# Right one-hots of a dense gate table: twelve tokens in one 16-bit compare, weighted by ScalarE and GpSimd

## What is computed

```
top_s, top_i = lax.top_k(s, 16)                       # s: (token, head, 2, 128)
cand_s = top_s[:, :, 0, :, None] + top_s[:, :, 1, None, :]
fs, fi = lax.top_k(cand_s.reshape(T, 8, 256), 16)
idx = take_along_axis(cand_i, fi)                     # cand_i = first * 128 + second
g = softmax(fs)
a = gelu(einsum('td,thkd->thk', x, u[idx]))
out = einsum('thk,thkd->td', g * a, v[idx])
```

## Time and profile before

| | us |
|---|---|
| median of 3 runs (lowest, highest) | 3995.82 (3994.71, 3996.32) |
| the profiled execution: its own time | 3995.24 |
| the profiled execution: span of its trace | 3993.4 |
| gate stage of layer 0, first DVE instruction of line 1615 to last copy of line 1449 | 780.73 to 892.96 |
| gate stage of layer 1, the same | 2790.94 to 2903.96 |

### The profile page before, as it was taken

One profiled execution on the slowest core, in us unless ns is written; L12 is line 12 of the kernel. 1 busy time (PEld: TensorE's weight loads), 2 busy tenths in 40 slices (PEclk: granted clock), 3 DMA queues, 4 the chain that ended last, 5 costly groups with the idle time before them and its releaser, 6 DMA issues. The chain is left out here.

```text
span 3993.4 us, 55792 instructions
## 1 busy us (share of the span) xinstructions
PE 3761.6 (94%) x20637; PEld 3189.9 (80%) x20637; DVE 3269.3 (82%) x6833; ACT 1769.7 (44%) x2928; POOL 989.6 (25%) x796
## 2 busy tenths in 40 slices
PE   8999999789999999999899898995989999999999
PEld 4546789588999999999754646894889999999998
DVE  5727549998999999999763435399979999999998
ACT  3316522394444444444324545222944444444443
POOL 0000000183333333333100000000933333333332
PEclk9999889799999999999989999897999999999999
DMA  7310030399999999999640000300999999999997
GB/s 294 137 44 10 22 126 2 116 260 424 415 415 408 405 407 404 404 405 404 256 158 22 22 22 19 128 1 22 229 404 415 413 410 406 405 404 405 405 405 299
DMA packets 268270, 1033.70 MB, mean 259 GB/s; under 512 B 147072, under 2 KB 150080, under 8 KB 159936
## 3 DMA queue, kind: packets, MB, share of 16 engines
q0 software_dynamic: 77184, 562.07, 35.1%
q1 hardware_dynamic: 190816, 468.07, 30.9%
HBM read 970.69 MB, written 59.39 MB: 258 GB/s over the span
## 5 line engine op out<-in xcount | busy, mean ns | idle before, releaser
L1696 POOL DMA_INDIRECT gbuf<-in_uv,rows x340 | 514.4, 1513 | 863.9 <-DVE hT L1880 794.1
L1488 POOL TENSOR_SCALAR pqT<-iota,selT 128x128 f32<-128x128 f32 x256 | 205.2, 815 | 1323.0 <-ACT selT L1430 1292.6
L1880 DVE SCALAR_TENSOR_TENSOR hT<-gbuf,act,hT 128x1024 f32<-128x1024 f32 x336 | 416.9, 1282 | 6.0
L1865 DVE SCALAR_TENSOR_TENSOR gbuf<-gbuf,ht 128x1024 f32<-128x1024 f32 x340 | 401.9, 1219 | 11.6 <-DMA gbuf<-in_uv,rows 11.6
L1696 POOL DMA_INDIRECT xT<-in_uv,rows x172 | 256.8, 1493 | 473.2 <-DVE hT L1880 393.4
L1712 PE MATMUL ps<-h0h,U0h 128*128 128x384 f32 x1024 | 344.8, 337 | 7.0 <-DVE U0l L1839 7.0
L1712 PE MATMUL ps<-h1h,U1h 128*128 128x384 f32 x1024 | 345.3, 337 | 6.3 <-DVE U1l L1839 6.3
L1712 PE MATMUL ps<-h1h,U1l 128*128 128x384 f32 x1024 | 344.5, 336 | 0.0
L1712 PE MATMUL ps<-h1l,U1h 128*128 128x384 f32 x1024 | 344.5, 336 | 0.0
L1712 PE MATMUL ps<-h0h,U0l 128*128 128x384 f32 x1024 | 344.5, 336 | 0.0
L1712 PE MATMUL ps<-h0l,U0h 128*128 128x384 f32 x1024 | 344.1, 336 | 0.0
(11 more groups left out here) (386 smaller groups left out, 9016.3 us busy)
## 6 DMA issues: line engine op xcount, KB each, us to landing
ring<-in_u SPq DMA_DIRECT2D x128, 1024.0 KB, 13.0
ring<-in_v SPq DMA_DIRECT2D x128, 1024.0 KB
ring<-in_wts SPq DMA_DIRECT2D x26, 2048.0 KB, 8.8
gates<-ring SPq DMA_DIRECT2D x32, 1536.0 KB, 7.4
ring<-gates SPq DMA_DIRECT2D x64, 768.0 KB
abuf<-in_ada_mid POOLq DMA_DIRECT2D x16, 1024.0 KB, 5.0
xT<-in_ada_late SPq DMA_DIRECT2D x16, 1024.0 KB, 4.9
abuf_c<-in_ada_late POOLq DMA_DIRECT2D x8, 1024.0 KB, 5.0
```

Of the source, the lines that this page charges most:

```text
L1488: last = pool.tensor_scalar(one2[:, r % 2, t, :], iota[:], selT[:, 1, t0 + t:t0 + t + 1], selT[:, 2, t0 + t:t0 + t + 1], ALU.is_equal, ALU ...
L1696: pool.indirect_dma_start(out=slots[m % GSLOTS], out_offset=None, in_=inp[f"uv{l}"], in_offset=bass.IndirectOffsetOnAxis(ap=rows[:, c:c + ...
L1865: v.scalar_tensor_tensor(u, u, 1.0, ht[:, m // P, :], ALU.mult, ALU.mult, accum_out=act4[:, n % 2, m % 2:m % 2 + 1]).then_inc(sem(n_ + "do ...
L1880: v.scalar_tensor_tensor(y, x, w, y, ALU.mult, ALU.add).then_inc(sem(n_ + "acc"), 1)
```

## The change

A new SBUF tensor `sel16` holds the second indices as f16, and a view `numbers` of the score buffer holds 0..127 as f16, each value 12 times over (so that the number is the outer and the token the inner index). One DVE instruction of a step compares all 12 tokens into a double buffer `hot` (a view of the old `eq`, f16) in the order partition, number, token. ACT weights tokens 0 to 3 and GpSimd tokens 4 to 11, each reading `hot` with a stride of 12 values and writing the f32 `one2`; GpSimd does its 8 tokens in one instruction. The compares of lines 1615, 1619 and 1488 go. The wait of TensorE for GpSimd moves behind its fourth product; DVE waits for ACT and GpSimd of step r-2 before it writes `hot`, and for the product of step r-2 only before the left one-hots; ACT waits for that product too.

```diff
 def expert_choice(...)
+        hot = eq[:].rearrange("p a h s k -> p (a h s k)")[:, 0:2 * P * SUB].rearrange("p (b n t) -> p b n t", b=2, n=P)
+        numbers = sc[:, 1].bitcast(F16).rearrange("p i k -> p (i k)")[:, 0:P * SUB].rearrange("p (n t) -> p n t", n=P)
-        SUB, DIRECT, SCALED = 12, 2, 6
+        SUB, SCALED = 12, 4
 TensorE, gate_step(r)
                     pe.wait_ge(sem("gm_one"), r + 1)
-                    pe.wait_ge(sem("gm_pool"), r + 1)
                     pe.wait_ge(sem("gm_scaled"), r + 1)
...
                     for t in range(SUB):
+                        if t == SCALED:
+                            pe.wait_ge(sem("gm_pool"), r + 1)
 ScalarE
                 def evict_sel(tb):
                     act.wait_ge(sem(n_ + "t"), tb + 1)
+                    act.copy(sel16[:, tb * P:(tb + 1) * P], ps[:, 5, P:2 * P])
...
                 def scaled(r):
                     act.wait_ge(sem("gm_eq"), r + 1)
-                    for t in range(DIRECT, DIRECT + SCALED):
-                        at = act.activation(one2[:, r % 2, t, :], one2[:, r % 2, t, :], ACT.Identity,
+                    if r >= 2:
+                        act.wait_ge(sem("gm_mm"), r - 1)
+                    for t in range(SCALED):
+                        at = act.activation(one2[:, r % 2, t, :], hot[:, r % 2, :, t], ACT.Identity,
                                             scale=selT[:, 2, r * SUB + t:r * SUB + t + 1])
...
+                act.copy(numbers, iota[:].unsqueeze(2).to_broadcast([P, P, SUB]))
                 act.copy(iota_ps, iota[:]).then_inc(sem("gm_iota"), 1)
 GpSimd
                 for r in range(STEPS):
-                    t0 = r * SUB
-                    pool.wait_ge(sem(n_ + "selT"), (t0 + SUB - 1) // P + 1)
+                    t0, n = r * SUB + SCALED, SUB - SCALED
+                    pool.wait_ge(sem("gm_eq"), r + 1)
                     if r >= 2:
                         pool.wait_ge(sem("gm_mm"), r - 1)
-                    for t in range(DIRECT + SCALED, SUB):
-                        last = pool.tensor_scalar(one2[:, r % 2, t, :], iota[:], selT[:, 1, t0 + t:t0 + t + 1],
-                                                  selT[:, 2, t0 + t:t0 + t + 1], ALU.is_equal, ALU.mult)
-                    last.then_inc(sem("gm_pool"), 1)
+                    pool.tensor_tensor(one2[:, r % 2, SCALED:SUB], hot[:, r % 2, :, SCALED:SUB].rearrange("p n t -> p t n"),
+                                       selT[:, 2, t0:t0 + n].unsqueeze(2).to_broadcast([P, n, P]), ALU.mult)\
+                        .then_inc(sem("gm_pool"), 1)
 VectorE, gate_step(r)
                     if r >= 2:
+                        v.wait_ge(sem("gm_scaled"), r - 1)
+                        v.wait_ge(sem("gm_pool"), r - 1)
+                    v.tensor_tensor(hot[:, r % 2], sel16[:, t0:t0 + SUB].unsqueeze(1).to_broadcast([P, P, SUB]),
+                                    numbers, ALU.is_equal).then_inc(sem("gm_eq"), 1)
+                    if r >= 2:
                         v.wait_ge(sem("gm_mm"), r - 1)
-                    n = SCALED
-                    v.tensor_tensor(one2[:, r % 2, DIRECT:DIRECT + n],
-                                    selT[:, 1, t0 + DIRECT:t0 + DIRECT + n].unsqueeze(2).to_broadcast([P, n, P]),
-                                    iota_ps.unsqueeze(1).to_broadcast([P, n, P]), ALU.is_equal).then_inc(sem("gm_eq"), 1)
-                    for t in range(DIRECT):
-                        v.tensor_scalar(one2[:, r % 2, t, :], iota_ps, selT[:, 1, t0 + t:t0 + t + 1],
-                                        selT[:, 2, t0 + t:t0 + t + 1], ALU.is_equal, ALU.mult)
                     v.tensor_tensor(one1[:, r % 2, 0:SUB], selT[:, 0, t0:t0 + SUB].unsqueeze(2).to_broadcast([P, SUB, P]),
                                     iota_ps.unsqueeze(1).to_broadcast([P, SUB, P]), ALU.is_equal)\
                      .then_inc(sem("gm_one"), 1)
```

More of the change, by code:

```diff
@@ L1269, in expert_choice @@
     def expert_choice(l, w3, pqT, keysT, selT, rows, gates, steps, sc, s2, cand, c2, vals, idxu, posu, idxp, ranks, posh,
-                      shift, fs, first, eq, tabs, sel, mrow):
+                      shift, fs, first, eq, tabs, sel, mrow, sel16):
         n_ = "ch_"
@@ L1931, in expert_layer @@
                               sb(s2, f"first{l}", [P, 2, 16, 16], F16), sb(s2, f"eq{l}", [P, 2, HP, 16, 16], F16),
-                              sb(s2, f"tabs{l}", [P, 2, HP, 16, 16], F16), sb(s2, f"sel{l}", [P, TB, 2, HP, 16]), sb(s2, f"mrow{l}", [P, 2, 256]))
+                              sb(s2, f"tabs{l}", [P, 2, HP, 16, 16], F16), sb(s2, f"sel{l}", [P, TB, 2, HP, 16]), sb(s2, f"mrow{l}", [P, 2, 256]),
+                              sb(s2, f"selT16{l}", [P, TD], F16))
             def pair(name, shape):
```

## The result

The changed kernel takes 4001.76 us (20 runs), the kernel before 3995.28 in the same comparison: 6.5 us more. The ratio is 1.0015, with a 95% interval of 1.0008 to 1.0022, so 3 to 9 us slower. That has the sign of the forecast and lies inside the range of 3979 to 4062, but it is a third of the size: it lies under the forecast's own range of 4004 to 4055, and within the 0.2% that I had called no change. (The period, 3.43 us, does lie in the 3.37 to 4.3 of the forecast.) The profiled execution has a span of 3999.9 us against 3993.4.

A forecast was written before the change was run, and what follows sets the result against it. In the gate stage all engines and DMA were near their limit; DVE and POOL taking turns would lengthen the period from 3.205 to 3.65 us, adding 10.9 x 2 = 21.8 us to 3995.82: 4018 us, range 3979 to 4062 (forecast's own 4004 to 4055).

The forecast's parts named there:

- Mechanism: Gate stage: POOL's reading and DVE's compare take turns, both reading SBUF; period 3.37 to 4.3 us, chance 0.42.
- POOL's reading: Gate step: DVE's next compare must wait until POOL has read, 2.6 us after POOL's start, at 2.6 ns a value.
- POOL's whole instruction: Gate step: GpSimd's single instruction of 1024 values with two inputs, one strided, takes 3.1 us.
- When POOL lets go: Gate step: DVE's compare can begin 2.6 us after POOL's start, before POOL's 3.1 us instruction ends.
- The sum: Gate stage: 24 steps at 3.65 instead of 3.205 us cost 10.7 us per layer, last six 0.2; 21.8 us in all.
- rival 2: Gate stage: POOL keeps DVE out for its whole duration; period 4.15 us, time 4048; chance 0.13.
- rival 5: Gate stage: compare at one value a cycle, 4066 us, or POOL as slow as eight single instructions, 4204; chance together 0.07.
- The start: Ahead of the gate stage and at its first products: added copies and PE's wait for POOL cost nothing.
- ACT's stride: Gate step: ACT's strided input costs nothing; four weightings at 0.31 us and the copy, about 2.6 us.
- The end: Gate stage's last six steps: 21.9 us against 21.7 imposed by stores; step 30's wait shrinks from 4.33 to about 2.
- Store loop: Gate stage: store landing, copies and weightings take 11.5 us for four steps, so no period under 2.9 us.
- Rival 3: Gate stage: the wait doesn't decide, reading plus compare falls under the store loop; period 2.9 us, time 3982; chance 0.26.

The follow-up runs named there:

- e1: The changed kernel with the compare's numbers 0..127 read from PSUM, so one operand in SBUF; 3989.78 us, ratio 0.9987 to the kernel before.
- e2: The changed kernel with GpSimd weighting only one of its eight tokens, the other seven left out; 3987.43 us, ratio 0.9981 to the kernel before.
- e10: e9 with the numbers 0..127 in PSUM as well; 3982.41 us, ratio 0.9966 to the kernel before.
- e3: The changed kernel with ACT and GpSimd reading `hot` without a stride (one-hots wrong, no work left out); 3981.04 us, ratio 0.9962 to the kernel before.
- e5: The kernel before, plus idle PE products ahead of the gate stage (32 in layer 0, 24 in layer 1); 3993.37 us, ratio 0.9995.
- e6: The changed kernel, plus the same idle PE products ahead of the gate stage as e5; 4000.76 us, ratio 1.0010 to the kernel before.
- e7: e1 with 3 tokens weighted by ACT and 9 by GpSimd; 3982.14 us, ratio 0.9964 to the kernel before.
- e9: The changed kernel with `hot` in three groups of four tokens, read at a stride of 8 bytes; 3980.48 us, ratio 0.9965 to the kernel before.

## Why the prediction was off

- **Mechanism: right.** DVE's compare and POOL's instruction take turns; each engine's own work fell and the period rose. Compare 0.95 us alone: measured 0.95. Handover 0.1: 0.09. Shown by e1, e2 and e10.
- **The term that failed: POOL's reading**, "0.28 + 896 x 0.0026 = 2.6 us", and with it the period of 3.65. Measured: DVE's work begins 2.40 us after POOL's start, and the period is 3.43. The price of 2.6 ns for two inputs with a stride came from no row; it is 2.31 ns (e2 and the changed kernel), and 0.28 + 896 x 0.00231 = 2.35 would have been nearly right. The bound of 2.2 ns from the 0.17 us delay was nearer, by luck, as it is of another instruction.
- **POOL's whole instruction**, "0.79 + 896 x 0.0026 = 3.1 us", measured 2.54. The 0.79 us of line 1488's compare-and-multiply was no fixed cost for this other form, whose 128 values take 0.475 us (e2).
- **When POOL lets go.** I had it let go 0.5 us before its end; it let go 0.14 before (2.40 of 2.54). It is 0.14 in e3 too, where the instruction takes 1.90: POOL starts at 821.54 and ends at 823.44, the compare of 823.05 takes 1.20, so its 0.95 us of work began at 823.30. Over all held compares of steps 2 to 30, in both layers, it is 0.13 to 0.14 us in either kernel. The Trainium skill's whole instruction (SBUF — State Buffer, Who interferes with whom) was nearer for this long one. With 2.54 it gives 2.54 + 0.95 + 0.09 = 3.58 us, against 3.43 measured. It was luck that 0.56 us too much for the instruction and 0.36 too much for the early release cancelled but for 0.2.
- **The sum.** At 3.43 instead of 3.65 the 24 steps cost 5.5 us instead of 10.7 in each layer; that is 10 of the 15 us by which I was too high. At the upper end I made a slip: rival 2 with 3.4 us for POOL's instruction has a period of 4.45 us and by the same sum comes to 4066, as rival 5, so 4062 does not take it in.
- **The start, "Nothing".** This was wrong, and is most of the other 5 us. I compared PE's first product and overlooked that before, DVE lost 2.8 us at step 2 to PE's half clock, while in the changed kernel it loses 0.2. So the copy of step 1 comes 11.0 us after the first compare instead of 12.2 in layer 0 (10.9 instead of 12.2 in layer 1). ACT, which was behind the turns by then, catches up: its next copies follow at 3.0 to 3.2 us for five steps before the period of 3.43 holds, another 1.3 us in each layer. e5 and e6 show it for layer 0.
- **ACT's stride, "costs nothing in my sum".** It costs 0.13 us an instruction. Leaving it out did no harm only because ACT had room; in e1 ACT set the pace.
- **The end.** 21.7 us from step 25 on, as forecast, in layer 0; 22.2 in layer 1. Step 30's copy waited 3.05 us, where I had said about 2. The row names PE, but the product of step 30 had ended at 886.97 + 2.92 = 889.89, and the copy came at 893.36. It was the store again: the one that SP had issued at 881.35 took 11.9 us and landed at 893.28. The DMA share, forecast below 0.9 in the steps, is 0.94.
- **PE's releaser.** I named POOL with 0.7 us; it is DVE's left one-hots with 0.5. The wait for POOL stands ahead of the fifth product, and with 2.54 instead of 3.1 us POOL was done by then: its instruction of 819.86 ended at 822.40, while PE, started at 821.72, came to its fifth product at 822.68.
- **Store loop, 2.9 us.** No mean period over steps 8 to 24 came under it; in e3 and e7 it was 2.98 to 3.11. Rival 3, at 3982, is what these runs reached: its condition, reading plus compare under the stores' pace, was met with 8 bytes of stride or with an operand in PSUM, not by the change as it stands.

## To carry to other kernels

Before moving an operand of a VectorE instruction from PSUM to SBUF, look at what GpSimd does at that time. Here, with two operands in SBUF, VectorE's compare had to wait until GpSimd had read, and GpSimd's next instruction waits for that compare by semaphore: nearly the sum of both durations became a bound. Work out such a bound between the two engines before counting what each one saves alone. And when a layout makes one engine's write dense and others' reads strided, choose the inner group so that the stride is 8 bytes, as in e9; here that turned 6 us of loss into 14 of gain.

## What was unexpected of the hardware

- A 16-bit compare of two tensors is as fast with one of them in PSUM: 0.947 us for 1536 values in e1, 0.951 with both in SBUF in e2. The f32 one of line 1625 takes 1.74.
- GpSimd's two-input instruction costs 0.18 us and 2.31 ns a value at a stride of 24 bytes, and 1.90 us for 1024 values at 8 bytes or none. ScalarE's weighting of 128 values takes 0.520 us at 24 bytes, 0.406 at 8 and 0.393 without a stride.
- GpSimd lets the held compare begin 0.13 to 0.14 us before its own instruction ends, whether that takes 2.54 us (changed kernel) or 1.90 (e3).
- DVE, held up by GpSimd, shows as a longer instruction, not as idle time (1.85 us for 0.95), so the engine looks 100% busy while 0.9 us of each 3.43 is waiting.
